# Inner norms of a hybrid decoder layer: token-wise sums of squares, three-column roots, and a new order of the first two products

## The reference, cut to what matters

```python
def _rmsnorm(x, g):
    y = x32 * lax.rsqrt(jnp.mean(x32 * x32, axis=-1, keepdims=True) + EPS)
    return (y * g).astype(x.dtype)
...
u = _modulate(_rmsnorm(x, norm_ff1), sh1, sc1)      # first norm
x = x + 0.5 * g1 * _swiglu(u, ff1_w1, ff1_w3, ff1_w2)
u = _modulate(_rmsnorm(x, norm_mix), sh2, sc2)      # second norm (norm 1)
... u @ w_in, mLSTM and SSD branches, merged @ w_out
x = x + g2 * (merged @ w_out)
u = _modulate(_rmsnorm(x, norm_ff2), sh3, sc3)      # third norm (norm 2)
x = x + 0.5 * g3 * _swiglu(u, ff2_w1, ff2_w3, ff2_w2)
```

## Time and profile before

| | |
|---|---|
| Time, median of 3 runs | 1338.71 us (1338.21 to 1343.4) |
| Profiled execution, its own time | 1340.6 us |
| Its span | 1338.9 us |
| Mean granted TensorE clock | 0.985 of full speed |
| PE busy / PEld busy | 1272.0 / 1157.1 us (95% / 86%) |
| DVE / ACT / POOL busy | 768.1 / 617.7 / 215.4 us |

### The profile page before, as it was taken

The page is one execution under the profiler, slowest core; times in us unless marked ns, Lnnn a source line. Parts: engine busy times, 40 slices in busy tenths (PEclk is TensorE's granted clock), DMA queues, the critical chain, the costliest instruction groups (busy, mean ns, idle before and its releaser), DMA issues. The chain is left out here.

```text
span 1338.9 us, 22662 instructions
## 1 busy us (share of the span) xinstructions
PE 1272.0 (95%) x9096; PEld 1157.1 (86%) x9096; DVE 768.1 (57%) x1340; ACT 617.7 (46%) x1066; POOL 215.4 (16%) x377
## 2 busy tenths in 40 slices
PE   6899999998999999989999999999999999999997
PEld 3799999997997776668998888888989979999997
DVE  1644445336885565655379786865665565545433
ACT  3433333334667554644355664554652343333443
POOL 3100000001540321211024242321500010000010
PEclk9899999998999999999999999999999989999999
DMA  9957677785443688893764355473436465544551
GB/s 301 265 182 230 221 221 212 224 235 179 127 127 127 199 273 291 290 282 106 203 196 128 119 173 167 134 213 114 126 94 189 142 205 158 154 137 131 152 149 42
DMA packets 258862, 241.56 MB, mean 180 GB/s; under 512 B 8607, under 2 KB 242479, under 8 KB 258710
## 3 DMA queue, kind: packets, MB, share of 16 engines
q1 hardware_dynamic: 249262, 211.03, 52.0%
q0 software_dynamic: 9024, 28.91, 6.3%
q10 hardware_dynamic: 472, 0.17, 0.1%
HBM read 209.88 MB, written 30.21 MB: 179 GB/s over the span
## 5 line engine op out<-in xcount | busy, mean ns | idle before, releaser
L2113 DVE TENSOR_TENSOR w_lo<-ring,w_hi 128x1024 fp32r<-128x1024 f32 (+1 forms) x264 | 336.8, 1277 | 421.1 <-ACT w_hi L1541 420.6
L1541 ACT ACTIVATE w_hi<-ring 128x1024 fp32r<-128x1024 f32 (+1 forms) x264 | 289.3, 1097 | 532.3 <-PE bank L826 526.2
L826 PE MATMUL bank<-u_hi,w_hi 128*128 128x320 f32 x1536 | 275.4, 323 | 9.6 <-ACT u_hi L1566 5.1
L826 PEld LDWEIGHTS bank<-u_hi,w_hi 128*128 128x128 f32 x1536 | 238.2, 193 | 28.3 <-issue 19.5
L826 PE MATMUL bank<-u_lo,w_hi 128*128 128x320 f32 x1536 | 257.6, 310 | 0.0
L826 PE MATMUL bank<-u_hi,w_lo 128*128 128x320 f32 x1536 | 257.0, 310 | 0.1
L826 PEld LDWEIGHTS bank<-u_lo,w_hi 128*128 128x128 f32 x1536 | 234.8, 189 | 0.0
L826 PEld LDWEIGHTS bank<-u_hi,w_lo 128*128 128x128 f32 x1536 | 233.7, 188 | 0.6 <-DVE w_lo L2113 0.4
L628 POOL TENSOR_TENSOR arena<-arena 128x320 f32<-128x320 f32 x24 | 21.0, 874 | 611.8 <-ACT arena L1553 598.8
L823 PE MATMUL aux<-ident,arena 128*128 128x128 f32 (+6 forms) x404 | 61.8, 278 | 17.3 <-ACT arena L1598 8.7
L826 PE MATMUL bank<-arena 32*128 32x128 f32 (+5 forms) x536 | 57.5, 376 | 15.1 <-DMA arena<-in_state_mlstm_C 7.9
(11 more groups left out here) (363 smaller groups left out, 1513.0 us busy)
## 6 DMA issues: line engine op xcount, KB each, us to landing
ring<-in_w_in SPq DMA_DIRECT2D x52, 1024.0 KB, 5.4
ring<-in_ff_w SPq DMA_DIRECT2D x44, 1024.0 KB, 5.5
ring<-in_ada_w SPq DMA_DIRECT2D x36, 1024.0 KB, 7.4
ring<-in_ff_w SPq DMA_DIRECT2D x32, 704.0 KB, 4.9
arena<-in_state_mlstm_C SPq DMA_DIRECT2D x32, 512.0 KB, 5.6
out_s_C<-arena POOLq DMA_DIRECT2D x32, 512.0 KB, 5.7
ring<-in_w_pa SPq DMA_DIRECT2D x8, 1024.0 KB, 8.1
arena<-in_state_ssm SPq DMA_DIRECT2D x32, 256.0 KB, 4.3
```

The source lines that it names most:

```text
L826: return nc.tensor.matmul(dst, lhs, rhs, start=first, stop=last)
L1541: nc.scalar.activation(w_hi[v.split_no % 2][:, 0:v.kc, :], panel_part(v), ACT.Copy).then_inc(S["hi_done"], 1)
L2113: V.tensor_tensor(w_lo[r][:, 0:v.kc, :], panel_part(v), w_hi[r][:, 0:v.kc, :].bitcast(FP32), ALU.subtract)\
```

## The change

Four things, in both inner norms:

1. The sum of squares is made token by token. `token_sums` uses 128 tokens of the squares as the stationary operand and one column of ones as the moving one, three times for the sum of tiles 0 to 6 and three times for tile 7. The result is three columns of aux[0], with tokens in the partitions: tokens 0 to 127, 128 to 255 and 192 to 319 (`TOKENS_AT`), the last so that the 64 sample tokens lie in partitions 64 to 127. Both halves now stand after the gap's first ada unit.
2. Root (`token_root`) and reciprocal act on these three columns (rs_t) instead of 320. There is one reciprocal instead of two.
3. `spread_roots` multiplies the columns, broadcast, with the identity: three fp32 matmuls that put the inverse roots of all 320 tokens in all partitions of aux[1]. VectorE reads them there. TensorE does this right behind the sums, ahead of the gap's other two ada units.
4. In `dense_two` the two units' w_lo products come ahead of the low tiles' products, and VectorE makes the pending w_lo ahead of the low halves of the norm.

The waits on `rr_mm` in the gated norm are counted one higher, since the second norm now uses that semaphore too.

```diff
+TOKENS_AT = (0, 128, T - 128)
...
+                for u in us:
+                    pe.wait_ge(S["lo_done"], u.split_no + 1)
+                    for kc in range(KD):
+                        mm(bank_of(u), w_lo[u.split_no % 2][:, kc, :], u_hi[:, kc, :], False, False)
                 for kc in range(KD):
                     pe.wait_ge(S["u_lo_ready"], low_at(norm, kc))
                     for u in us:
-                        mm(bank_of(u), w_hi[u.split_no % 2][:, kc, :], u_lo[:, kc, :], False, False)
-                for u in us:
-                    pe.wait_ge(S["lo_done"], u.split_no + 1)
-                    for kc in range(KD):
-                        ins = mm(bank_of(u), w_lo[u.split_no % 2][:, kc, :], u_hi[:, kc, :], False, kc == KD - 1)
-                    ins.then_inc(unit_done, 1)
+                        ins = mm(bank_of(u), w_hi[u.split_no % 2][:, kc, :], u_lo[:, kc, :], False, kc == KD - 1)
+                        if kc == KD - 1:
+                            ins.then_inc(unit_done, 1)
...
+            def token_sums(n):
+
+                pe.wait_ge(S["sq_summed"], n + 1 if n < 2 else n + SG + 1)
+                for c in range(3):
+                    mm(aux[0][:, c:c + 1], sq[:, 0, TOKENS_AT[c]:TOKENS_AT[c] + 128], ones[:, 0:1], c == 0, False)
+                pe.wait_ge(S["sq_ready"], (n + 1) * KD)
+                for c in range(3):
+                    ins = mm(aux[0][:, c:c + 1], sq[:, KD - 1, TOKENS_AT[c]:TOKENS_AT[c] + 128], ones[:, 0:1], False, c == 2)
+                ins.then_inc(S["sumsq_done"], 1)
+
+            def spread_roots(n):
+
+                pe.wait_ge(S["inverse_ready"], n + 1)
+                for c in range(2):
+                    mm(aux[1][:, c * 128:(c + 1) * 128], rs_t[:, c:c + 1].to_broadcast([128, 128]), ident[:, :])
+                mm(aux[1][:, TP:T], rs_t[64:128, 2:3].to_broadcast([64, 128]), ident[64:128, 64:128]).then_inc(S["rr_mm"], 1)
...
-            sum_squares_most(1)
             for u in st.range(("ada", ADA_GAP2[0]), ("ada", ADA_GAP2[-1])):
                 ada(u)
                 if before and before.name == "ada":
                     mod_columns(before)
                 if u.q == ADA_GAP2[0]:
-                    sum_squares_last(1)
+                    token_sums(1)
+                    spread_roots(1)
                 before = u
...
+            def token_root(n):
+                act.wait_ge(S["sumsq_done"], n + 1)
+                nc.scalar.activation(rs_t[:, 0:3], aux[0][:, 0:3], ACT.Sqrt, bias=eps_col[:, 0:1], scale=1.0 / D).then_inc(S["root_ready"], 1)
...
             def gap_norm(n, shift, fill, second):
 
                 dve.wait_ge(S["root_ready"], n + 1)
-                ch.link(V.reciprocal(rs[:, TP:T], rs[:, TP:T]))
+                V.reciprocal(rs_t[:, 0:3], rs_t[:, 0:3]).then_inc(S["inverse_ready"], 1)
                 dve.wait_ge(S["us_ready"], 4 + n)
-                ch.link(V.tensor_tensor(xg_s[:, :, :], xg_s[:, :, :], rs[:, None, TP:T].to_broadcast([128, KD, TS]), ALU.mult))
+                dve.wait_ge(S["rr_mm"], 1 if n == 1 else SG + 2)
+                ch.link(V.tensor_tensor(xg_s[:, :, :], xg_s[:, :, :], aux[1][:, None, TP:T].to_broadcast([128, KD, TS]), ALU.mult))
                 V.tensor_tensor(u_t[:, :, TP:T].rearrange("p k (b t) -> p k b t", t=ST), xg_s[:, :, :].rearrange("p k (b t) -> p k b t", t=ST),
                                 mod_of(shift)[:, :, 1:NSEQ].unsqueeze(3).to_broadcast([128, KD, SB, ST]), ALU.add).then_inc(S["xr_ready"], 1)
-                V.reciprocal(rs[:, 0:TP], rs[:, 0:TP]).then_inc(S["inverse_ready"], 1)
-                dve.wait_ge(S["inverse_ready"], n + 1)
-                normed(0, KD)
+                normed(0, KD, aux[1])
+                low_ahead(fill[-1], second)
                 samples_low(n, 0, KD)
                 tiles_low(n, shift, 0, KD)
-                low_ahead(fill[-1], second)
                 for u in fill:
                     mod_add(u)
```

More of the change, by code:

```diff
@@ L1480, in _ @@
                 before = u
-            sum_squares_most(2)
             before = None
@@ L1488, in _ @@
                 if u.q == ADA_GAP3[0]:
-                    sum_squares_last(2)
+                    token_sums(2)
+                    spread_roots(2)
                 before = u
@@ L1659, in _ @@
             ada_row(fill[0])
-            root(1)
+            token_root(1)
             high_ahead(fill[0], st.at["qk", 1])
@@ L2053, in _ @@
             act.wait_ge(small_out, (2 + 2 * MH) * 16)
-            root(2)
+            token_root(2)
             high_ahead(fill[0], st.at["up2", 1])
@@ L2132, in inverse_root, with normed @@
                 dve.wait_ge(S["inverse_ready"], n + 1)
-            def normed(first, end):
+            def normed(first, end, inverse=rs):
                 for kc in range(first, end):
-                    V.scalar_tensor_tensor(out=u_t[:, kc, 0:TP], in0=x_t[:, kc, 0:TP], scalar=gain[:, kc, 0:1], in1=rs[:, 0:TP],
+                    V.scalar_tensor_tensor(out=u_t[:, kc, 0:TP], in0=x_t[:, kc, 0:TP], scalar=gain[:, kc, 0:1], in1=inverse[:, 0:TP],
                                            op0=ALU.mult, op1=ALU.mult).then_inc(S["xr_ready"], 1)
@@ L2726, in group_norm @@
                 gr = c // 4
-                dve.wait_ge(S["rr_mm"], gr + 1)
+                dve.wait_ge(S["rr_mm"], gr + 2)
                 V.scalar_tensor_tensor(out=xbc_t[:, c, :], in0=xbc_t[:, c, :], scalar=par[:, 200 + c:201 + c], in1=aux[1 + gr % 3][:, 0:T],
```

## The result

The changed kernel is slower: 1342.85 us median against 1338.51 (20 runs each), ratio 1.0032, interval 1.002 to 1.0044. Two further sets of twelve runs gave 1.0045 (1.0029 to 1.0062) and 1.0042 (1.0023 to 1.006). That is 4.3 to 6 us, outside the predicted range. The profiled execution happens to be the shortest of its twenty (own time 1336.45, span 1334.7), so its span says nothing: its first dense product began 2.8 us sooner than that of before (38.70 against 41.48), and from the one inner norm to the other, where the work is the same, it took 747.0 us where the one of before took 754.6. TensorE's granted clock fell there four times in the profile of before (13.6 us at 1.2 GHz in all), and not once in this one. What counts is read inside the changed stretches, from landmark to landmark.

A forecast was written before the change was run, and what follows sets the result against it. TensorE, busy 95% of the span, was taken as the bound, so only its idle time and low clock count. Gaps -0.2 and -0.25, w_hi +0.95, clock -0.5: total 0.0, forecast 1338.7 us, range 1335.6 to 1341.5.

The forecast's parts named there:

- The fill moved onto ScalarE's chain: First gap: ada units queue behind the spread, their row copies ahead of the tiles; of 1.6 us won, 0.2 reaches TensorE.
- The w_hi wait behind the third norm: Behind the second gap's first two units: their group closes 7 matmuls later, so TensorE waits for w_hi, 0.95 us lost.
- No wait for u_lo in either gap: Low tiles come later but stay hidden, by 1.2 us in the second gap; rival of a wait, with the rest, 0.03.
- PSUM as the source cost nothing: VectorE reads inverse roots from PSUM at no cost; the skill's rule would add about 0.6 us a gap.
- Sums, root, spread: From last square to first high tile in each gap: 0.2 us gained in the first, 0.25 in the second.
- the clock in the fill: Ada units between spread and high tiles in both gaps: priced at full clock, 1.01 us each, with no fall priced there.
- With 1.01 for each and 0.36 for the turn between: First gap: times for ada 30 and 31 and the turn between, so ada 31 is issued by 317.4.
- of the 3.2 us I take 0.5 back: Low clock costs 3.2 us in both gaps; shorter idle time returns 0.5, between all of it and a loss of 1.8.
- Rival (b): In the gaps the clock falls in the middle of the tiles, its slow stretch covering only full work: 1341.0, chance 0.17.
- the head: The first norm's pair of units at the kernel's start; the prediction had no term for it.
- The part on the order of the products: Low weights first in both gaps: takes no wait away, adds 0.95 us in the second gap, none in the first.

The follow-up runs named there:

- rows_late: The changed kernel with ScalarE's copy of each gap's last ada row moved behind the high tiles; ratio to before 0.9999 (0.9988 to 1.0011).
- after_again: The changed kernel, unaltered, timed and profiled a second time; ratio to before 1.0045 (1.0029 to 1.0062).
- head_only: The kernel before with the new product order in the first norm's pair alone, at the kernel's start; ratio 1.0018 (1.0 to 1.0037).
- head_old: The changed kernel with the first norm's pair, at the kernel's start, in the old product order; 1342.6 us, ratio 1.0033 (1.0017 to 1.005).
- warm: The changed kernel with two unneeded products ahead of the last three sums and two ahead of the spread in each gap; 1342.36 us, ratio 1.0024.
- warm_again: The same kernel as warm, timed and profiled once more; 1343.0 us, ratio 1.0028 (1.0011 to 1.0045).
- pairs_warm: The changed kernel with old product order, last ada row copied behind the tiles, both units' high products tile by tile, unneeded products in the waits; 1333.72 us, 0.9964.

## Why the prediction was wrong

**Right, by the profile.** The fill moved onto ScalarE's chain: ScalarE idle for 2.10 us ahead of its last ada row copy, and the first high tile right behind; rows_late shows it by moving the copy behind the tiles. The w_hi wait behind the third norm: 0.95 us forecast, 0.93 in the profile (the third unit starts 1.32 us behind the turn's start, before 0.30: 1.0 lost); none behind the second norm. No wait for u_lo in either gap. PSUM as the source cost nothing: the eight scaled tiles took 3.21 us, before 3.26; the Trainium skill's 120 against 58 cycles ("VectorE: DVE Perf Modes", the TRN2 errata) is not what these rows show.

**Sums, root, spread: -0.2 and -0.25 us at full clock.** Measured at full clock, in the third norm's gap: +0.14 (tile 5.94 or 5.95 against 5.81). No second norm's gap of these kernels had its fill at full clock. The mis-sized terms show in after_again's third norm, TensorE, ScalarE and then VectorE there:

```profile
1085.95 1.50 PE L827 MATMUL aux<-ones,arena 128*128 128x1 f32 x12
1088.14 1.07 PE L827 MATMUL aux<-ident,stats 128*128 128x128 f32 x6 [0.69 <-DVE stats L2276]
1089.15 1.07 PE L827 MATMUL bank<-ring,c_t 128*32 128x256 f32 x16
```

```profile
1086.04 0.47 ACT L1572 ACTIVATE arena<-x_t 128x320 f32<-128x320 f32 x1 [2.75 <-DVE x_t L2206]
...
1087.55 0.26 ACT L1580 ACTIVATE stats<-aux,eps_col 128x3 f32<-128x3 f32 x1 [0.77 <-PE aux L827]
```

```profile
1087.91 0.17 DVE L2276 RECIPROCAL stats<-stats 128x3 f32<-128x3 f32 x1 [1.91 <-ACT stats L1580]
1089.33 0.69 DVE L2279 TENSOR_TENSOR arena<-arena,aux 128x512 f32<-128x512 f32 x1 [1.24 <-PE aux L827]
...
1090.66 3.21 DVE L2160 SCALAR_TENSOR_TENSOR arena<-x_t,gain,aux 128x256 f32<-128x256 f32 x8
```

The square ends at 1086.51. The root starts 1.04 us later where the prediction had 0.80: three one-column products take 0.83 us, not 0.65. The spread takes 1.07 us, not 0.97, and is done at 2.70 us where it had 2.25, so the next ada unit starts 2.64 us behind the square where it had 2.20. Most of that 0.44 us passes through the last ada row to the first high tile and turns 0.25 gained into 0.14 lost. The first scaled tile comes at 4.15 us where it had 3.55: 1.1 us sooner than before, not 1.6. The hand-overs from root to reciprocal to spread took what the prediction gave them.

**The step that failed: the clock in the fill.** "With 1.01 for each and 0.36 for the turn between" prices ada 30 and 31 at full clock, and "of the 3.2 us I take 0.5 back" lets the fall move only on the pair's products. I asked whether the old fall would be saved, not whether the new pattern (one-column products and short waits) would let one come ahead of the fill. Before, a slow fill would have been hidden all but about 0.3 us (an estimate: the earlier trace rows with the 2.48 us from one ada unit to the next and the 2.0 to the copy that the changed kernel shows at 1.2 GHz); I had just moved it onto the chain. Two ada units and a turn at 1.2 GHz, in some gaps the spread too, put the tile at 7.4 to 8.7 us. Against before, it is 1.9 us later in the mean of twelve gaps. Rival (b) had the right sign and named the clock, but put the fall in the tiles and had 1341.0 as its price.

**The step that is missing: the head.** The part on the order of the products counts two gaps; `dense_two` has three callers. The two waits there (0.54 and 1.15 us, 1.8 to 1.9 us in all with their hand-overs) were to be read in the code and the trace of before: VectorE's last w_lo there runs from 46.74 to 47.95, and with the new order TensorE wants it eight matmuls behind 46.12, at 47.3. head_only shows it in its stretch, +1.9 us; its time, 1.0018 (1.0 to 1.0037), agrees, and head_old's doesn't resolve it.

Added up for the changed kernel: head 1.9, its two gaps +4.5, +3.1 and +2.7 us in the three profiled executions (3.4 in the mean), 5.3 in all; the ratios say 4.3 to 6.0. The own times of those three executions say less, 1.6 us over the two of before in the mean, since their stretch between the norms was 3.2 us shorter in the mean. So the sum agrees with the times of the many runs, and a part that differs from one execution to the next is larger than any one term of it. What makes a fall come in one execution and not in the next was not tried; that the timing varies is what the Trainium skill says ("TensorE: Matmul & The Clock Gate", Part 1), and the three executions of one kernel agree with it.

## What to carry to other kernels

Work that fills a wait is free only while it lies beside the chain: when a change puts a wait ahead of it, price the fill again, at the low clock too. Look at which copies of it stand ahead of the chain's work in the other engines' queues. Look up every caller of a function whose order you change, since an order that is harmless where both inputs are ready stalls where one is made last. When a group of matmuls closes later, the buffer it reads comes free later: ask what is made in that buffer next, and what covers it.

## What the runs showed of the hardware

Idle time is not all that comes ahead of a fall of the granted clock. In the kernels with one-column sums and no filler it stood at 1.2 GHz in 15 of 20 fills, in the changed kernel's first profile from the end of the second norm's last sums on, after a wait of 0.74 us; with the old sums of 320 columns, behind a wait of 1.33 us in the profile of before, in none of twelve. With the same weight loads and 128 columns (waits of 0.56 and 0.63 us) it was none of two, and with filler products in the waits one of six (warm, warm_again, pairs_warm). Which of the two, the columns or the waits, decides isn't shown. The 128 columns cost 0.94 instead of 0.83 us for three products. And the clock can rise and fall again within one gap: in the changed kernel's profile 0.50 from 312.4 to 319.2, 1.00 until 322.6, 0.50 again until 326.0.
